# Gate products of eleven strip pairs as seven half-block products, kept in DRAM, with the branch products in a stage behind them

## The reference, cut to what matters

```
branches = einsum('btgc,gcd->btgd', stack([out_a, out_b, out_c]), w_branch)   # 3 x (1024x512 @ 512x1024)
gates    = sigmoid(h @ w_gate + b_gate).reshape(b, t, 3, 1024)                # 1024x1024 @ 1024x3072
x        = x + sum(gates * branches, axis=2) @ w_out                          # 1024x1024 @ 1024x1024
```

## Time and profile before

| What | us |
|---|---|
| Median of 3 runs | 3132.02 |
| Lowest and highest run | 3129.63, 3132.77 |
| Span of the profiled execution | 3129.0 |
| TensorE busy in it | 3066.4 (98%) |
| VectorE busy | 1791.4 (57%) |
| ScalarE busy | 1329.6 (42%) |
| GpSimd busy | 664.3 (21%) |

### The profile page before, as it was taken

One profiled execution on the slowest core, in us unless ns is written; L12 is line 12 of the kernel. 1 busy time (PEld: TensorE's weight loads), 2 busy tenths in 40 slices (PEclk: granted clock), 3 DMA queues, 4 the chain that ended last, 5 costly groups with the idle time before them and its releaser, 6 DMA issues.

```text
span 3129.0 us, 50323 instructions
## 1 busy us (share of the span) xinstructions
PE 3066.4 (98%) x18600; PEld 2608.8 (83%) x18600; DVE 1791.4 (57%) x3573; ACT 1329.6 (42%) x2637; POOL 664.3 (21%) x886
## 2 busy tenths in 40 slices
PE   7999999999999999999999999998999999999999
PEld 7988888999999888888788888888977777787777
DVE  6657674353344322345888887876353666753675
ACT  5446565454445221232333333454433555522552
POOL 3423334453542000001111111001101011032240
PEclk9999999999999999999999999999999999999999
DMA  5110011011111321122233225643100000221012
GB/s 204 37 48 18 21 35 51 28 62 44 56 59 46 103 78 51 45 95 97 72 109 109 102 101 204 196 151 140 46 28 22 16 28 15 108 72 67 28 61 101
DMA packets 77412, 231.27 MB, mean 74 GB/s; under 512 B 17712, under 2 KB 21936, under 8 KB 65648
## 3 DMA queue, kind: packets, MB, share of 16 engines
q1 hardware_dynamic: 77168, 228.05, 20.8%
HBM read 183.92 MB, written 43.84 MB: 73 GB/s over the span
## 4 chain that ended last, share of the span: by engine, by line
PE 90%; DVE 6%; ACT 2%; issue 1%; DMA 1%; SPq 0%; POOL 0%; DVEq 0%; ACTq 0%; POOLq 0%
PE ps L2546 71%; PE ps L2589 7%; PE ps L2597 3%; PE ps L2553 2%; PE ps L2604 2%; PE ps L2620 2%; PE ps L2612 1%; PE ps L2623 1%; PE ps L2640 1%; DVE wlo L2815 0%; DVE hlo L2892 0%; ACT hhi L2660 0%; ACT whi L2650 0%; DVE qk L2923 0%; DMA fa2r<-scratch_fs 0%
## 5 line engine op out<-in xcount | busy, mean ns | idle before, releaser
L2546 PE MATMUL ps<-whi,hhi 128*128 128x256 f32 (+2 forms) x1920 | 580.5, 302 | 3.0 <-DVE hlo L2892 1.7
L2546 PE MATMUL ps<-whi,hlo 128*128 128x256 f32 (+2 forms) x1920 | 563.7, 294 | 0.0
L2546 PE MATMUL ps<-wlo,hhi 128*128 128x256 f32 (+2 forms) x1920 | 563.4, 293 | 0.0
L2546 PEld LDWEIGHTS ps<-whi,hhi 128*128 128x128 f32 x1920 | 368.2, 192 | 12.8 <-issue 5.1
L2546 PEld LDWEIGHTS ps<-wlo,hhi 128*128 128x128 f32 x1920 | 368.8, 192 | 7.4 <-issue 0.2
L2546 PEld LDWEIGHTS ps<-whi,hlo 128*128 128x128 f32 x1920 | 368.2, 192 | 7.7
L2546 PE MATMUL ps<-hhi,whi 128*128 128x512 f32 x864 | 342.3, 396 | 0.0
L2546 PE MATMUL ps<-hhi,wlo 128*128 128x512 f32 x864 | 337.0, 390 | 0.0
L2546 PE MATMUL ps<-hlo,whi 128*128 128x512 f32 x864 | 336.3, 389 | 0.0
L3154 POOL TENSOR_SCALAR stats<-stats 128x2 f32<-128x2 f32 (+2 forms) x230 | 59.3, 258 | 1194.1 <-ACT xsf L2654 509.1
L3143 POOL CAST whi<-raw 128x512 fp32r<-128x512 f32 (+4 forms) x180 | 113.7, 631 | 865.8 <-PE ps L2546 856.1
(11 more groups left out here) (616 smaller groups left out, 6996.6 us busy)
## 6 DMA issues: line engine op xcount, KB each, us to landing
raw<-in_W SPq DMA_DIRECT2D x61, 1024.0 KB, 4.8
scratch_fs<-fo SPq DMA_DIRECT2D x77, 256.0 KB, 2.0
raw<-in_W SPq DMA_DIRECT2D x24, 768.0 KB, 4.3
wd<-in_WD SPq DMA_DIRECT2D x44, 256.0 KB, 3.5
wf0b<-in_WF SPq DMA_DIRECT2D x10, 1024.0 KB, 5.3
wf1b<-in_WF SPq DMA_DIRECT2D x10, 1024.0 KB, 5.2
scratch_x<-x SPq DMA_DIRECT2D x16, 512.0 KB, 3.3
orw<-scratch_outs SPq DMA_DIRECT2D x6, 1024.0 KB, 5.8
```

Of the source, the lines that this page charges most:

```text
L2546: x = e.matmul(r.out, a, b, start=(r.start and m == 0), stop=(r.stop and m == n - 1), skip_group_check=r.joined)
```

## The change: seven products in place of eight for eleven pairs, and the branch products afterwards

The 24 gate strips are paired, strip x with strip x + 12 in the order of `GATE_STRIPS`. The first pair is multiplied as before, but in eight pieces of 12 matmuls. Each of the other eleven pairs is a 2x2 block of weights (2 strips by 2 halves of the 1024 input features) times a 2x2 block of h (2 halves of features by 2 halves of tokens), and is computed with 7 products of 12 matmuls in place of 8. The sums of h (gt3, gt2, gt4, gt1; four blocks each, handled as two combines and two splits of 128x1024 a step) are made on VectorE while attention B ends and during pair 1. Each gate tile gets its tanh (`gate_out`) and is stored to DRAM. After pair 11 the branch products run alone, 12 chunks of 2 strips by 2 halves, and load the gate tiles back. The branches' split outputs now lie in parts of `hhi` and `hlo`, and `mix_split` follows each pair of tiles in the last branch.

```diff
-    for g in GATE_ORDER:
-        for d in range(8):
-            add(("w_gate", 0, 8, [(g * 1024 + d * 128, 128)]), ("w_branch", g * 512, 4, [(d * 128, 128)]))
+    add(("w_gate", 0, 8, [(128 * GATE_STRIPS[x], 128) for x in (0, GATE_PAIRS)]))
+    held = [len(plan)]
+    for g in GATE_ORDER:
+        for c in range(4):
+            add(("w_branch", g * 512, 4, [(256 * c, 256)]))
...
+        def gate_out(src_, x, hf, ready, outs, free, j, place=None, at_=0):
+            ...
+            emit("gate_out", r)
+            gate_kept[x, hf] = store(f"fs{at_ + j}", d["gates"][x, :, 512 * hf:512 * hf + 512], outs[j], r.done)
+            free[j] = [gate_kept[x, hf]]
...
+        def gate_front():
+            s, b_last = gsets[1], b_vlast[0]
+            s.load(0, b_last, b_fin[2, 3], qk_n_free)
+            yield
+            next(gate_piece)
+            yield
+            gsets[0].load(1, b_last, spl_done[held[0] - 1])
+            yield
+            next(gate_piece)
+            s.sums(0, b_last)
+            yield
+            s.split(0, 0, free=b_last)
+            yield
+            for x, c in enumerate(g_two):
+                near = [b_units[55].v_full, b_units[55].s_full, b_units[55].exps]
+                combine(False, gt3[:, c, :], b_at(g_hi, 1, late, c), b_at(g_hi, 0, late, c), ALU.subtract, near)
+                combine(False, gt3[:, c, :], gt3[:, c, :], b_at(g_lo, 1, late, c), ALU.add)
+                yield
+                next(gate_piece)
+                three[x] = combine(False, gt3[:, c, :], gt3[:, c, :], b_at(g_lo, 0, late, c), ALU.subtract)
+                s.split(0, (2, 1)[x], free=b_last)
+                yield
+            s.split(0, 5, free=b_last)
+            yield
+            for x, c in enumerate(g_two):
+                two[x] = combine(False, gt2[:, c, :], gt3[:, c, :], b_at(g_hi, 0, early, c), ALU.add, b_units[63].s_full)
+            yield
...
-                if n in (4, 9):
-                    next(gate_gen)
+                next(gate_gen, None)
                 yield
...
+        next(gate_piece)
+        s = GatePair(1)
+        for x, c in enumerate(g_two):
+            g_read["t3"].append(op_split(gt3[:, c, :], gt3h[:, c, :], gt3l[:, c, :], three[x], two[x], near))
+        for x, c in enumerate(g_two):
+            two[x] = combine(False, gt2[:, c, :], gt2[:, c, :], b_at(g_lo, 0, early, c), ALU.add)
+        four = [combine(False, gt4[:, c, :], b_at(g_hi, 1, early, c), gt2[:, c, :], ALU.subtract, b_read, gp_free) for c in g_two]
+        for x, c in enumerate(g_two):
+            g_read["t2"].append(op_split(gt2[:, c, :], gt2h[:, c, :], gt2l[:, c, :], two[x], four[x], b_read))
+        for _ in range(3):
+            next(gate_piece)
+        drain(gate_piece)
+        s.p1()
+        s.keep()
+        t1_free = [g_plain[0], g_plain[1]]
+        s.p7()
+        for c in g_two:
+            out = gt1[:, c, late]
+            combine(False, out, b_at(g_hi, 0, late, c), b_at(g_hi, 0, early, c), ALU.subtract, t1_free)
+            combine(False, out, out, b_at(g_lo, 0, late, c), ALU.add)
+            one = combine(False, out, out, b_at(g_lo, 0, early, c), ALU.subtract)
+            g_read["t1"].append(op_split(out, hlo[:, c, late], hhi[:, c, late], one, None, None))
+        s.p2()
+        s.out11()
+        s.p6()
+        s.u3()
+        gsets[1].split(0, 4, 3, free=b_vlast[0])
+        s.p5()
+        for x, c in enumerate(g_two):
+            four[x] = combine(False, gt4[:, c, :], gt4[:, c, :], b_at(g_lo, 1, early, c), ALU.add)
+            g_read["t4"].append(op_split(gt4[:, c, :], gt4h[:, c, :], gt4l[:, c, :], four[x], None, b_read))
+        gsets[1].split(0, 6, free=b_vlast[0])
+        s.out22()
...
+        s.p3()
...
+        s.p4()
...
+        for i in range(2, GATE_PAIRS):
+            last_m = s.m3.full if i > 2 else s.m4.full
+            s, here, other = GatePair(i), gsets[i % 2], gsets[1 - i % 2]
+            more = i + 1 < GATE_PAIRS
+            if more:
+                other.sums(i)
+            else:
+                w_late[0] = 0
+                w_release([[last_m], None], [[last_m], None], 1)
+                w_split()
+            s.p1()
+            s.keep()
+            here.split(i - 1, 6)
+            s.p6()
...
+            s.p2()
+            s.p7()
...
+            s.out11()
+            s.p5()
+            s.u3()
+            if more:
+                other.split(i, 0, 5)
+            s.p4()
+            if i + 2 < GATE_PAIRS:
+                here.load(i + 1)
+            s.out22()
...
+            s.p3()
+            s.out21()
...
+            s.out12()
...
+        for gi in range(3):
+            for c in range(4):
+                ch = Chunk()
+                for y in range(2):
+                    for hf in range(2):
...
+                        gm["branch"] = mm3(r.branch, r.branch.ps[:, :], lhs, rhs, 4, ch.split, o_made[gi, hf])
...
+                        emit("gate_mix", r)
...
+                        tile_load()
+                    if gi == 2 and dd:
+                        for hf in range(2):
+                            mix_split(hf, dd - 1)
+                ch.done(gm["branch"])
```

More of the change, by code:

```diff
@@ L31 @@
 GATE_ORDER = (0, 2, 1)
+GATE_PAIRS = 12
+GATE_STRIPS = [8 * g + d for g in GATE_ORDER for d in range(8)]
 SPLIT_PARTS = 2
@@ L1116, in build @@
         a_done = [u.fin, u.v_full, u.exps[-1], u.s_full, t_outA]
-        mix = rest("mix", [8, T], F, 16 * KB)
-        orw = rest("orw", [4, T], F, 0)
-        ohi = rest("ohi", [4, T], R, 48 * KB)
-        olo = rest("olo", [4, T], R, 64 * KB)
-        scr = Slots([rest(f"scr{i}", [512], F, (80 + 2 * i) * KB + 512) for i in range(4)])
-        mix_done, mix_rows, gm = {}, {}, {"branch": None}
-        def mix_split(hf, *ks):
-            for k in ks:
-                mix_rows[k, hf] = split_half(mix, 0.5, k, hf, mix_done[k, hf], gm["gate"])
@@ L1188, in build, with combine @@
-        osp = []
-        gate_gen = gates()
+        early, late = sl(0, 512), sl(512, 512)
+        of = lambda *kb: [RAW + n * KB for n in kb]
+        of_rest = lambda *kb: [REST + int(n * KB) for n in kb]
+        def combine(by_pool, out, a, b, op, *after):
+            r = Rec()
+            r.by_pool, r.out, r.a, r.b, r.op, r.after = by_pool, out, a, b, op, flat(*after)
+            r.done = signal("sum_pool" if by_pool else "sum_dve")
+            emit("combine", r)
+            return r.done
@@ new lines, in product_of, with ff_add @@
+        def product_of(s, i, ops, ready, p, place, joined=False):
+            j, name = FF_WEIGHT[p - 1], FF_FIRST[p - 1]
+            lhs = [(lambda k, w=w: w[:, 128 * k:128 * k + 128]) for w in (s.of(i).hi[j], s.of(i).lo[j])]
+            s.done[j] = mm3(place, place.ps[:, :], lhs, ops[name], 4, s.made[j], ready[name], start=not joined, joined=joined)
+            return place
+        def ff_add(out, place, other, *free):
+            r = Rec()
+            r.out, r.place, r.other, r.free = out, place, other, flat(*free)
+            emit("ff_add", r)
+            return place.read
@@ new lines, in plain_gates @@
+        def plain_gates():
+            ch = Chunk()
+            for n, (x, hf) in enumerate(((0, 1), (1, 1), (0, 0), (1, 0))):
+                p = DB.take()
+                for a in (0, 4):
+                    m = mm3(p, p.ps[:, :], views(ch.part(0), sl(128 * x, 128)), views(hpair, sl(512 * hf, 512)), 8, ch.split,
+                            last=a == 4, blocks=[(k, None) for k in range(a, a + 4)], start=a == 0, stop=a == 4)
+                    if a == 4:
+                        if n < 2:
+                            gate_out(p.ps[:, :], GATE_PAIRS * x, hf, p.full, gp_raw, gp_free, n, p, 4)
+                        else:
+                            gate_out(p.ps[:, :], GATE_PAIRS * x, hf, p.full, go, go_free, n, p)
+                        g_plain[n] = m
+                    yield
+            ch.done(m)
@@ new lines, in build @@
+        gsets[0].split(1, 0, free=g_slot)
+        s.p3()
+        gsets[0].split(1, 5, free=g_slot)
+        s.p4()
+        gsets[0].split(1, 1, 2, free=g_slot)
+        s.out21()
+        s.out12()
+        gsets[1].load(2)
+        gsets[0].split(1, 4, 3, free=g_slot)
+        mix = rest("mix", [8, T], F, 16 * KB)
+        orw = [rest(f"orw{i}", [4, 512], F, (8 - 8 * i) * KB) for i in range(2)]
+        ohi = rest("ohi", [4, T], R, 48 * KB)
+        olo = rest("olo", [4, T], R, 64 * KB)
+        o_place = [lambda w, o, hf, c: w[:, 4 * hf + c, early], lambda w, o, hf, c: w[:, 4 * hf + c, late],
+                   lambda w, o, hf, c: o[:, c, sl(512 * hf, 512)]]
@@ L1433, in build @@
         t4h, t4l = [rest(n, [4, 512], R, (64 + 8 * i) * KB) for i, n in enumerate(("t4h", "t4l"))]
-        early, late = sl(0, 512), sl(512, 512)
         h_ops = {
@@ L1587, in product @@
         def product(i, p, place, joined=False):
-            s, j, name = sets[i % 2], FF_WEIGHT[p - 1], FF_FIRST[p - 1]
```

(12 more changed lines are left out.)

367 lines of the change are left out of this document (231 added, 136 removed).

## The result

The changed kernel takes 3138.34 us (median of 11 runs, 3136.46 to 3140.48), the kernel before 3131.77 us (11 runs on the same chip). The ratio is 1.0022, with a 95% interval from 1.0014 to 1.0031: 6.6 us slower, a small change but with an interval clear of 1. It is 11 us above the forecast of 3127, and 0.3 us above the upper end of the stated range, 3138. The profiled execution has a span of 3134.5 us and took 3136.46, the shortest of the 11.

The account below looks back on a forecast made before the run. TensorE, busy 98% of the span, was taken as the bound. The terms -29.9 + 18.8 + 2.5 + 0.5 + 1.7 + 1.6 = -4.8 us gave 3124.2 for the profiled execution, 3127 us as median, range 3110 to 3138 (8 in 10).

Parts of the forecast that it names:

- 132 matmuls fewer: Gate pairs: eleven pairs go from 96 to 84 matmuls at 0.2267 us each, all on the path, -29.9 us.
- In front of pair 1, with its clock: Attention B's end through pair 1: TensorE waits for VectorE's queue, 18.8 us, plus 2.5 us of half clock.
- Pair 2: Second gate pair: some 0.5 us of waiting, because b_merge stands ahead of the add on VectorE.
- Into the branch stage: Pair 11: product 2 waits 1.7 us for its bank, the copy keep standing behind a branch chunk's split.
- End of the branch stage: Last branch tiles: VectorE runs late, so blocks 6 and 7 of the mix make TensorE wait 1.6 us.
- What is removed: Gate pairs: 132 matmuls go at the trace's 0.2267 us each, saving 29.9 us if nothing else moves.
- The front: Attention B's end to pair 1's end: one VectorE backlog costs 18.8 us, including 7.0 in the attention.
- Rival B: Combines from 1002 to 1063: at 2.4 us each they add 22.8 us, giving 3150 us; chance 0.10.
- D: Gate pairs: the seven products are not fewer matmuls on TensorE; chance 0.01.
- rival A: VectorE's queue from 1002 to 1063: better cover returns 10 to 13 us, giving 3116 us; chance 0.33.
- C: Pairs slip on late loads, 1 us a pair, 10 us in all, 3137 us; 0.09 with others above 3134.
- Pairs 2 to 11: Steady gate pairs: VectorE needs 11.6 us of 19.05 a pair, no TensorE wait except some 0.5 us in pair 2.

Follow-up runs that it names:

- e4_late: Changed kernel with the second half of gt3's combines made later, at step 10 of attention B's last twelve, behind the weights b_weights: 3140.75 us.
- e9_merge: Changed kernel with both b_merge of attention B's last head moved behind pairs 3 and 4, the second one's weight load with it: 3130.87 us.
- f4_all_turn: Changed kernel with e5_inter, e9_merge, e1_keep and e6_osplit together, and ScalarE making all transposed-block copies in the last twelve attention steps: 3110.61 us.
- e5_inter: Changed kernel with pair 2's products 1, 6, 2 interleaved into pair 1, gt1 and gt4 combined before splitting, earlier load(2), last b_merge behind pair 3: 3124.48 us.
- e2_load: Changed kernel with pair 3's weights loaded directly behind product 4 of pair 1, ahead of two gate-tile stores in SyncE's queue: 3135.57 us.
- e1_keep: Changed kernel with the first branch chunk's split in pair 11 issued behind product 1 and its copy, not ahead of them: 3132.53 us.
- e6_osplit: Changed kernel with e1_keep's edit, and the split of out_a's first half in pair 11 put ahead of product 4: 3131.67 us.
- e7_pipe: Changed kernel with VectorE's and ScalarE's work in pair 1 reordered, gt1's six combines before its splits, weight 4's split ahead of the adds: 3135.04 us.
- e3_nolow: Changed kernel without the twelve 128x1024 combines that bring h's low parts into gt1 to gt4, so coarser gates: 3128.09 us.

## Why the prediction was wrong

| Term of the sum | Forecast | Measured |
|---|---|---|
| 132 matmuls fewer | -29.9 | -29.9 |
| In front of pair 1, with its clock | 18.8 + 2.5 | 24.6 |
| Pair 2 | 0.5 | 4.9 |
| Into the branch stage | 1.7 | 8.3 |
| End of the branch stage | 1.6 | 0 |
| Sum | -4.8 | +7.9 |

The measured terms are pair 1's end at 1074.38 less 1049.8; 23.94 less 19.04; 1408.58 - 1250.64 less 19.04 and 130.6. Their sum differs from the 7.76 us between the two stage ends by rounding only. Of the 12.7 us of error, 6.6 lie in the step into the branch stage, 4.4 in pair 2, 3.3 in the front, and -1.6 at the end.

**What is removed** was right: the spacing of the earlier trace rows held, and 84 matmuls take 19.04 us. So the page that would have made the saving an estimated 17.3 us (the Trainium skill, "TensorE: Matmul & The Clock Gate", "Back-to-back issue gap") is not borne out here either. By it the sum would have been +7.8, just what the stage lost, but by luck: it puts the miss where none was.

**The front** was right in mechanism, place and order: the last values end near 1029.5 (forecast 1026.9), product 5 starts at 1056.35 (1053.9) and product 3 at 1066.00 (1063.2), ended by just the rows named. Product 5 is 2.5 us late by VectorE's own waits for ScalarE and TensorE inside the queue. I had counted those behind gt1 and gt4; the others up to product 5 are seven of 0.3 to 1.5 us and sum to 4.4 us, against the 1 us that I had added and the 0.9 us by which the sums of weights began early (1001.20). Product 3 is 2.8 us late, and the clock behind it cost 2.9 where I had 2.5. e4_late shows that the stall in the attention is the same backlog, e9_merge and f4_all_turn that less of VectorE's work brings the end forward, e5_inter that the waits in front of products 5 and 3 can be covered. Rival B (combines at 2.4 us) and D are out by 1.225 us and by the count; of rival A the cover was not there; of C, pairs 3 to 10 took 19.04 us each and didn't slip.

**Pairs 2 to 11: "No wait, except some 0.5 us in pair 2" failed.** I took the load of pair 3's weights at the place of a steady pair. In pair 1 it stands behind two stores on SyncE, which wait for the tanh of `out21` and `out12`, and was issued at 1077.42; the sums could not start before 1082.50, and merge and add came behind. e2_load (0.58 us of wait) and e9_merge (none) show it. Of the 4.9 us, 2.98 are the wait and 1.9 the half clock behind it.

**"Into the branch stage", 1.7 us, failed most.** I had the right queue, `keep` behind the split of a branch chunk, but put the load 2.0 us into the pair and the landing 3.3 behind it, by a row that is a store's. It was issued at 1254.79, 4.15 us in, since `out12`, its tanh and its store come first, and the split ran at 1258.91, 4.1 us later. The wait was 4.04 us, near the 4 that I gave as the bound for wait and clock together, and the half clock, 2.1 us here, came on top. e1_keep gives 5.8 us back. And I had no term at all for `o_split` between `out22` and `out12`, 2.20 us in front of the first branch matmul, which e6_osplit takes away at its place. The measured 8.3 is rather low: from pair 3 to the end of the branch products the changed kernel's profile has 310.26 us, and the six others with the same code there (e2_load, e7_pipe, e3_nolow, e4_late, e9_merge, e5_inter) have 312.98 to 313.88.

**The end of the branch stage** cost nothing: VectorE was late as forecast (its last add of block 7 at 1412.45), but TensorE didn't wait.

So what failed were the two transitions between steady states, which I timed with the steady state's offsets: 11.0 of the 12.7 us. The term at the end of the branch stage was wrong the other way. Of the 11.8 us of clock, 7.8 lie in the front, where VectorE's queue held the end and only what lay behind product 3 counted, as I had said; the 4.0 in the two transitions had no term in the sum.

## What to carry to other kernels

A stage with fewer matmuls pays at its two ends: list there every queue, SyncE's too, in the order in which it was emitted, and time each load from the store that it stands behind, not from the steady state. When an engine's queue is the bound of a short stretch, the first thing to look for is independent work for TensorE to run meanwhile (here the waits in front of products 5 and 3 fell from 4.02 and 4.17 us to 0.25 and none, with no work removed); taking work off the queue is second, and moving it later can lose, since waits that it had filled come open. A small copy or tanh that frees a bank should never stand behind something that waits for a load or for another engine's long queue.
